# A two-layer backbone block on one core: order of routing, list loads and shared-expert steps

## The reference, cut to what matters

```python
def moe_ffn(h, w_router, router_bias, w_eg, w_eu, w_ed, w_sg, w_su, w_sd):
    scores = jax.nn.sigmoid((h @ w_router).astype(jnp.float32))
    # group-limited top-8 of 64, weights normalised, rows sorted by expert and padded to blocks of 128
    ...
    y = lax.map(expert_block, (row_tok.reshape(n_blocks, MOE_BLOCK), block_e)).reshape(n_rows, D)
    routed = jnp.zeros((T + 1, D), h.dtype).at[row_tok].add(y * row_w[:, None])[:T]
    shared = (jax.nn.silu(h @ w_sg) * (h @ w_su)) @ w_sd
    return routed + shared
```

## Time and profile before

| | |
|---|---|
| median of 3 runs | 3443.66 us (3431.37 to 3446.03) |
| the profiled execution | 3404.99 us, span 3403.1 us |
| PE busy | 3183.9 us (94%) |
| DVE, ACT, POOL busy | 1747.7, 1336.2, 595.3 us |
| chain that ended last, by engine | PE 68%, DMA 17%, DVE 5%, issue 4%, ACT 3%, POOL 1% |
| granted PE clock over the span | 0.981 |

### The profile page before, as it was taken

One profiled execution on the slowest core, in us unless ns is written; L12 is line 12 of the kernel. 1 busy time (PEld: TensorE's weight loads), 2 busy tenths in 40 slices (PEclk: granted clock), 3 DMA queues, 4 the chain that ended last, 5 costly groups with the idle time before them and its releaser, 6 DMA issues.

```text
span 3403.1 us, 47594 instructions
## 1 busy us (share of the span) xinstructions
PE 3183.9 (94%) x14840; PEld 2229.5 (66%) x14840; DVE 1747.7 (51%) x2409; ACT 1336.2 (39%) x1881; POOL 595.3 (17%) x751
## 2 busy tenths in 40 slices
PE   6999998999989999999998799999998899999996
PEld 3467866899645776667666346776764566776663
DVE  1344252133265766666675526342335666677665
ACT  2244152212122555555554225242212455555551
POOL 0000310000042332223332000020003222332220
PEclk9999999999999999999999999999999999999998
DMA  6310203333515999999996910103341899999986
GB/s 234 110 62 7 78 1 106 130 130 130 201 40 191 372 375 365 363 377 382 371 378 261 361 51 1 35 1 112 93 158 46 296 374 352 359 369 357 346 322 249
DMA packets 224802, 727.19 MB, mean 214 GB/s; under 512 B 55890, under 2 KB 104660, under 8 KB 165396
## 3 DMA queue, kind: packets, MB, share of 16 engines
q1 hardware_dynamic: 179508, 633.37, 50.6%
q0 software_dynamic: 45184, 92.28, 7.3%
HBM read 707.64 MB, written 84.24 MB: 233 GB/s over the span
## 4 chain that ended last, share of the span: by engine, by line
PE 68%; DMA 17%; DVE 5%; issue 4%; ACT 3%; POOL 1%; SPq 1%; DVEq 0%; POOLq 0%; ACTq 0%
PE ps L820 11%; PE ps L822 10%; PE ps L821 10%; PE ps L813 7%; PE ps L901 6%; DMA ring<-in_w_exp_up 6%; PE ps L842 5%; PE ps L1010 5%; DMA region_k<-in_w_exp_up 4%; PE ps L1112 4%; DMA region_v<-in_w_exp_up 3%; PE ps L1033 3%; DMA ring<-y_rows 2%; PE ps L929 1%; PE ps L1131 1%
## 5 line engine op out<-in xcount | busy, mean ns | idle before, releaser
L842 PEld LDWEIGHTS ps<-con,region_c 128*128 128x128 f32 x1878 | 249.0, 169 | 130.3 <-issue 90.8
L1967 POOL DMA_INDIRECT y_rows<-region_q,idx_out x141 | 147.3, 1045 | 892.2 <-DVE region_q L1572 806.4
L842 PE MATMUL ps<-con,region_c 128*128 128x128 f32 x1878 | 278.3, 277 | 22.0 <-DVE region_c L1803 8.7
L822 PE MATMUL ps<-region_x_split,ring_split 128*128 128x384 f32 (+2 forms) x800 | 283.9, 355 | 0.0
L820 PE MATMUL ps<-ring_split,region_q_split 128*128 128x512 f32 x568 | 227.9, 401 | 10.7 <-DVE ring_split L1539 8.7
L820 PE MATMUL ps<-region_h_split,region_q_split 128*128 128x512 f32 x560 | 225.1, 402 | 12.6 <-DVE ring_split L1539 11.7
L1190 ACT ACTIVATE region_q<-ps 128x512 f32<-128x512 f32 (+1 forms) x145 | 87.6, 604 | 366.7 <-PE ps L901 320.3
L822 PE MATMUL ps<-ring_split 128*128 128x512 f32 x568 | 222.6, 392 | 0.0
L822 PE MATMUL ps<-region_h_split,ring_split 128*128 128x512 f32 x560 | 220.1, 393 | 0.0
L1367 ACT ACTIVATE region_c<-ps 128x768 f32<-128x768 f32 (+1 forms) x48 | 33.8, 705 | 409.4 <-PE ps L822 409.4
L901 PE MATMUL ps<-region_k,region_c 128*128 128x512 f32 x384 | 172.8, 593 | 1.0 <-DVE region_c L1551 1.0
(11 more groups left out here) (312 smaller groups left out, 6886.0 us busy)
## 6 DMA issues: line engine op xcount, KB each, us to landing
ring<-in_w_mod SPq DMA_DIRECT2D x24, 2048.0 KB, 8.2
region_k<-in_w_exp_gate SPq DMA_DIRECT2D x48, 1024.0 KB, 7.4
region_k<-in_w_exp_up SPq DMA_DIRECT2D x48, 1024.0 KB, 16.8
region_k<-in_w_exp_down SPq DMA_DIRECT2D x48, 1024.0 KB, 15.3
ring<-in_w_exp_gate SPq DMA_DIRECT2D x47, 1024.0 KB, 7.6
ring<-in_w_exp_up SPq DMA_DIRECT2D x47, 1024.0 KB, 16.9
ring<-in_w_exp_down SPq DMA_DIRECT2D x47, 1024.0 KB, 15.3
region_v<-in_w_exp_gate SPq DMA_DIRECT2D x46, 1024.0 KB, 7.4
```

What stands on the lines that cost most here:

```text
L822: last = mm(o, wl, xh, start=False, stop=k == len(stationary) - 1)
L842: last = nc.tensor.transpose(ps[0:t.shape[1], at:at + t.shape[0]], t, ident[0:t.shape[0], 0:t.shape[0]])
L1967: pool.indirect_dma_start(Y8, bass.IndirectOffsetOnAxis(ap=idx_out[:, s:s + 1], axis=0), yb[:, s, :], None, bounds_check=TOK * TOPK - 1, o ...
```

## The change

In both layers, pieces 12 to 19 are split one `qs` step earlier (after `qs` 0 and 1, `qsp` 0 and 1, not after 1 and 2), and SP requests the first two merge panels before it waits for `rows`, not after. In both layers SP waits for the list stores and requests the lists ahead of the wait for the table and of all expert weights. Second layer: `r` of a tile stands before the next tile's `o`, `pos` directly a step later, POOL writes the lists two steps behind `keep_rows` rather than three, and the shared expert's jobs stand in a new order with `shift` last. First layer: the shared expert's jobs stand in a new order.

```diff
             if kind in ("qs", "qsp"):
-                return {1: [12, 13, 14, 15], 2: [16, 17, 18, 19]}.get(a[1], [])
+                return {0: [12, 13, 14, 15], 1: [16, 17, 18, 19]}.get(a[1], [])
...
-                load_until(("pm", l))
+                load_until(("merge", l, 1, 0))
                 sp.wait_ge(drained["dve"], names["rows", l].count)
...
                     spread("gt2", s, s_gt2)
+                sp.wait_ge(sl["listed"], 16 * TOPK * len(A))
+                sp.dma_start(slots, LISTS[l].rearrange("(p n) a -> p (n a)", p=P)).then_inc(sl["list_in"], 16)
                 sp.wait_ge(tab_ready, l + 1)
...
                 load_down(expert(1), 1)
-                sp.wait_ge(sl["listed"], 16 * TOPK * len(A))
-                sp.dma_start(slots, LISTS[l].rearrange("(p n) a -> p (n a)", p=P)).then_inc(sl["list_in"], 16)
                 sp.wait_ge(filled, names["sd", l, A[-1]].fill)
...
-                for n in range(len(A) + 3):
+                lag = 3 if l < DEPTH - 1 else 2
+                for n in range(len(A) + lag):
                     if n < len(A):
                         keep_rows(n)
-                    if n >= 3:
-                        list_tile(n - 3)
+                    if n >= lag:
+                        list_tile(n - lag)
```

More of the change, by code:

```diff
@@ L217, in make_plan @@
         assert not rest
+        router = dict(drain="act", panel=("router", l))
+        ahead = l == DEPTH - 1
         for i, t in enumerate(A):
+            if ahead and i >= 2:
+                add("r", l, A[i - 2], **router)
             add("o", l, t, drain="dve", panel=[("wo", l, 0), ("wo", l, 1)])
@@ L222, in make_plan @@
             add("norm", l, t)
[L223 to L227, removed]
-        add("f", l, A[-1], drain="act")
[L229 to L249, removed]
@@ L250, in make_plan, with shared @@
-        if l < DEPTH - 1:
+            if ahead and i >= 2:
+                add("pos", l, A[i - 2], drain="dve")
+            elif i >= 2:
+                add("r", l, A[i - 2], **router)
+                if i >= 3:
+                    add("pos", l, A[i - 3], drain="dve")
+        def shared(*steps):
+            for kind, n in steps:
+                add(kind, l, A[n], drain="act" if kind == "sT" else "dve")
+        if ahead:
+            add("r", l, A[-2], **router)
+        shared(("sg", 0))
@@ new lines, in make_plan @@
+        add("f", l, A[-1], drain="act")
+        if ahead:
+            shared(("pos", -2), ("sT", 0), ("sd", 0))
+            add("r", l, A[-1], **router)
+            shared(("sg", 1))
+        else:
+            add("r", l, A[-2], **router)
+            shared(("pos", -3), ("sT", 0), ("sd", 0))
+            add("r", l, A[-1], **router)
+            shared(("pos", -2), ("sg", 1), ("sg", 2))
+        shared(("pos", -1))
+        add("cnt", l, drain="dve")
+        shared(("sT", 1), ("sd", 1))
@@ L251, in make_plan @@
+        add("end", l, drain="dve")
+        shared(("sg", 2 if ahead else 3))
+        add("tab", l, drain="dve")
+        shared(("sT", 2), ("sd", 2))
+        if not ahead:
+            add("shift", l)
+            shared(("sg", 4), ("sT", 3), ("sd", 3))
+        add("first", l)
+        shared(("sg", -1))
+        if ahead:
+            add("shift", l)
+        else:
+            shared(("sT", -2), ("sd", -2))
             add("tok", l)
-        add("sT", l, A[-1], drain="act")
-        add("sd", l, A[-1], drain="dve")
@@ L254, in make_plan @@
-        if l == DEPTH - 1:
+        shared(("sT", -1), ("sd", -1))
+        if ahead:
             add("tok", l)
```

## The result

| timing | before, us | changed, us | difference | ratio, with its 95% interval |
|---|---|---|---|---|
| first | 3437.51 (4 runs) | 3377.52 (4 runs) | 60.0 | 0.9824 (0.9801 to 0.9846) |
| second (e5) | 3407.94 (19) | 3363.83 (4) | 44.1 | 0.9873 (0.9851 to 0.9895) |
| third (e10) | 3411.59 (28) | 3367.53 (4) | 44.1 | 0.9869 (0.9851 to 0.9886) |
| fourth (e14) | 3413.07 (9) | 3372.22 (2) | 40.9 | 0.9877 (0.9849 to 0.9906) |

A forecast was written before the change was run, and what follows sets the result against it. PE, busy 94% of the span, was taken as the bound, with gains from closing its gaps ahead of the expert loops: 14.0 + 14.8 + 5 + 6.5 = 40.3 us off the 3443.7 median gives 3403.4 us, range 3390 to 3423.

The forecast's parts named there:

- splits: Both layers, ahead of `u` 0: earlier splits close PE's gap and keep the clock up, 14.0 us (9.7 to 14.0).
- merge panels: Both layers, `pm` to `b`: earlier panel requests let `b` start as `pm` ends, 14.8 us (10.4 to 14.8).
- first layer's shared stage: First layer's shared expert jobs: new order fills PE's waits for `route` and `cnt`, 5 us (-3 to 8).
- second layer's routing and shared stage: Second layer: earlier list stores and list request end PE's wait for the lists sooner, 6.5 us (1 to 8).
- The 1.9 us that the prediction left at `r` 5: First layer's shared stage: a gap of about 1.9 us stays, as `r` 5 needs the slot of `pos` 3.
- waits of `r` 2 to 4: Second layer's routing: each waits for ACT's copy, about 4 us new; over 2 us each would show the prediction wrong.
- the walk through the queues to `pos` 5: Second layer's routing: places `pos` 5 at about 2622, so the last list store goes out at 2631, 10.7 us sooner.
- The bracket at `sT` 5: Second layer: `sT` 5 following a weight wait was a right sign; several us with a DMA behind, a wrong one.
- A: Rival: both shared stages give nothing, late expert weights or gathers replacing the gaps; 3414.9 us, chance 0.12.
- B: Rival: the early splits fail, through a late panel or another wait at `u` 0; 3417.4 us, chance 0.06.
- C: Rival: the expert loops lengthen, slower than before from 0.29 us a block; 3466.9 us at 0.45; chance 0.05.
- the last one, from the sum to the median: Whole kernel: 40.3 us taken off the 3443.7 median too, though the profiled execution lay an unplaced 38.7 us under it.

The follow-up runs named there:

- e5: The whole change again, against the kernel before: 3363.83 against 3407.94 us, ratio 0.9873.
- e10: The whole change again, on a third chip, against the kernel before: 3367.53 against 3411.59 us, ratio 0.9869.
- e14: The whole change once more, two runs, against the kernel before on the same chip: 3372.22 against 3413.07 us, ratio 0.9877.
- e11: First layer's new job order and lists ahead of expert weights, in the kernel before: 3406.44 against 3411.59 us, ratio 0.9982.
- e12: Second layer's new order with shorter list-store lag, and lists ahead of expert weights, in the kernel before: 3402.68 against 3411.59 us, ratio 0.9973.
- e1: The kernel before, unchanged, timed and profiled again: 3407.52 against 3408.39 us, ratio 0.9999.
- e13: The kernel before, unchanged, timed and profiled once more: 3411.22 against 3413.07 us.
- e6: Only the first layer's new job order, in the kernel before: 3411.64 against 3407.94 us, ratio 1.0019.
- e8: The whole change with `first` moved behind `sT` 5 in the second layer, against the kernel before: 3359.15 against 3407.94 us, ratio 0.9864.
- e3: The whole change without the earlier splits and merge panel requests, against the kernel before: 3390.45 against 3408.39 us, ratio 0.9948.
- e7: Only the second layer's new job order and shorter list-store lag, in the kernel before: 3405.24 against 3407.94 us, ratio 0.9992.
- e4: Only the lists requested ahead of the table and expert weights, in the kernel before: 3408.02 against 3408.39 us, ratio 0.9998.

## Why the prediction was right or wrong

**The sum.** The forecast's own range was 18 to 45 us of gain before the spread of the median; three later timings give 44.1, 44.1 and 40.9. Term by term:

| term | forecast, us | timed alone | in the stages |
|---|---|---|---|
| splits | 14.0 | 28.6 with the next | first layer 7.6 (forecast 7.56) |
| merge panels | 14.8 | | first layer 6.7 (6.57); second, both terms, 14.0 (14.70) |
| first layer's shared stage | 5 (-3 to 8) | 5.2 (e11) | 92.6 to 84.0: 8.6 |
| second layer's routing and shared stage | 6.5 (1 to 8) | 8.9 (e12) | 171.9 to 167.6: 4.3 |

The stage column takes means of the four profiles before and of e5, e10 and e14; its terms sum to 7.6 + 6.7 + 14.0 + 8.6 + 4.3 = 41.2. Against the one profile of before that the prediction was worked out from, the same differences are 7.7 + 6.1 + 14.4 + 7.0 + 5.1 = 40.3 us, the forecast itself. That is in part luck: the two shared stages are off by +2.0 and -1.4.

**Splits and panels: right.** Gap and clock went together, as summed: `u` 0 and `b` have no bracket and run at the durations of the full clock. What is lower behind a gap is again seen where one stayed: behind 4.89 us at `sT` 5 the eight matmuls of `sd` 5 take 5.15 us (2634.78), where they take 3.67 behind a gap of 0.56. By the Trainium skill's "TensorE: Matmul & The Clock Gate", section "What's actually happening", the point of transition varies from run to run; for the gaps removed here that mattered little, as the stage of the splits takes 102.9 to 103.4 us with its gap and 95.56 to 95.58 without. Elsewhere it mattered. In the second layer `sT` 2 starts 115.4 us behind the request for `w_out` in both e5 and e14. In e5 the `sg` 2 before it ran at a granted clock of 1.00, PE then idled 2.86 us, and `sd` 2 ran at 0.57; in e14 these are 0.84, 1.18 us and 1.00. `sd` 2 in e5, then in e14:

```profile
2576.32 6.38 PE L1160 MATMUL ps<-region_v,region_c 128*128 128x512 f32 x8 [0.56 <-ACT region_c L1205]
```

```profile
2576.75 3.67 PE L1160 MATMUL ps<-region_v,region_c 128*128 128x512 f32 x8 [0.57 <-ACT region_c L1205]
```

**First layer's shared stage: right in mechanism, under-sized by 2.0 us.** By the prediction the lists would be requested at 1040 to 1041 in before's time, expert 0 right behind. In e5 they are at 1026.99 and 1028.92; the stage begins 12.76 us earlier there (971.08 against 983.84), so 1039.75 and 1041.68. The expert weights were covered by `sg` 4 to `sg` 5 as reasoned: PE has no wait on a DMA in the stage, and the 3.07 us that ACT waits for them hold nobody up. PE's only bracket over 1.4 us is one of 3.30 ahead of `r` 4, which stood in the kernel before too (3.31 in e1). The 1.9 us that the prediction left at `r` 5 are not there: `sd` 0 covers them. With them the 5 us would have been 6.9, and from the profile of before (91.0 us) to the 84.0 it is 7.0. The 8.6 of the table are more because e1 and e13 are in its mean, at the lower clocks named with the stages. The experiments add what the prediction didn't weigh: this order alone wins nothing and is slower by 3.7 us as timed (e6). That the table comes later was noted there only as a cost for the weights; it also puts the lists behind them.

**Second layer: the wait moved, as said, and less was left over.** The waits of `r` 2 to 4 are 3.3 + 1.2 = 4.5 us, forecast 4. Behind them the chain runs as forecast, 2 to 5 us later. In before's time (the starts of `w_out` laid on 2492.13):

| step | forecast | e5 | e10, e14 |
|---|---|---|---|
| last list store | 2631 | 2635.9 | 2632.9, 2632.9 |
| lists requested | 2633 to 2634 | 2638.0 | 2635.1, 2635.1 |
| expert 0 requested | 2635.5 | 2640.5 | 2637.6, 2637.6 |
| PE behind its wait, at `sT` 5 | 2650.5 | 2654.1 | 2651.2, 2651.1 |

Against the 2656.98 of before, 2.9 us of the 6.5 are seen at this point in e5, and 5.8 and 5.9 in e10 and e14; in the first profile it is at 2657.3 and nothing is won. The mis-sized step is the walk through the queues to `pos` 5, put at 2622: POOL can store its rows at 2627.0 in e5 and at 2624.1 in e10 and e14. From e14 to e5 the difference is the slow `sd` 2 shown above. (The prediction calls the job at 2656.98 `sT` 4; by the order of the list it is `sT` 5, so it is the same job on both sides and the 6.5 stand.) PE waits for the second gather at `tok`, 1.52 us in the first profile, 1.42 and 1.36 in e5 and e10, and not at all in e14; the prediction only had 2 us less to spare there. The bracket at `sT` 5 was named, among the signs of right and also of wrong; it is 4.76 to 4.89 us, and e8 shows what makes it.

**Rivals.** A (the shared stages give nothing) falls by e3, 17.9 us; the late gathers of the first layer are not seen either, as `tok` waits 1.32 us for DVE before and after, and for no DMA. B falls by `u` 0, which has no bracket. C falls by the loops: 793.9, 792.6 and 794.5 us against 793.0 to 795.0, and 681.2, 679.8 and 683.2 against 679.3 to 683.4; a block would have had to be 0.29 us longer, 22 us in the first loop.

**The step that failed** is the last one, from the sum to the median: "So I take the same 40.3 off the median", with the 38.7 us between profile and median left unplaced and taken to fall on both kernels alike. It did not. Over the later timings the kernel before takes 3408 to 3413 us and the changed one 3364 to 3372; in the first, 3437.5 and 3377.5. So whatever made the first timing longer cost before 24 to 30 us and the changed kernel 5 to 14. The gain that the terms sum to is there, 41 to 44 us in the later timings; of the 25.9 us that the forecast missed by, 19.7 are the gain that only the first timing has, and 6.2 the starting value. The range, 54 us of gain at most, was built from the bounds of the terms and 5 us for the median, and had nothing for this.

What it was is only partly seen. The first profile of the changed kernel belongs to that timing, and its two shared stages, 89.63 and 172.3 us, are the longest of the four. There ScalarE starts late with no releaser on this core to name. ACT in the first layer, first profile, and then the same steps in e5:

```profile
1001.53 0.22 ACT L1405 ACTIVATE scores<-ps 128x64 f32<-128x64 f32 x1 [10.59 <-remote]
...
1011.56 0.38 ACT L1409 ACTIVATE region_c<-ps 128x256 f32<-128x256 f32 x1 [8.50 <-remote]
```

```profile
993.89 0.22 ACT L1405 ACTIVATE scores<-ps 128x64 f32<-128x64 f32 x1 [8.26 <-PE ps L1139]
...
1000.99 0.38 ACT L1409 ACTIVATE region_c<-ps 128x256 f32<-128x256 f32 x1 [5.57 <-PE ps L1146]
```

The same two steps are 2.3 and 2.9 us later behind their predecessors, and DVE and PE wait for them (PE 1.40 us at `sT` 1 and 2.78 at `sd` 1, against 0.55 and 0.61 in e5). No other profile has such a row, of either kernel. Why the kernel before lost more than twice as much there, and whether in these same places, stays open: no profile of it from that timing exists, and in no later timing did it take 3430 us. That the difference is one of chips is a guess: three chips gave 3408 to 3413, and which one the first timing ran on is not on record.

## What to carry to other kernels

An order of jobs and the order of a queue that serves them are one change: in the first layer the new order alone lost 3.7 us, the lists ahead alone won nothing, and together they won 5.2. When a step is moved, work out for every queue what now goes out ahead of what, and only then price the gap. And if a profile's own time doesn't lie among the timed runs, the unplaced difference is a term of its own, which need not be the same for both kernels, and the range must hold it.

## What the runs showed of the hardware that was not expected

- A load of the lists asked for right behind 6 MB of weights is usable 12.7 us (e6) and 13.1 us (e7) later; asked for some 12 us behind them it took 4.0 us (2647.64 to 2651.60), and with no weights asked for ahead of it 2.4 (e4 and e11, second layer). The Trainium skill, "Trainium Kernel Development and Optimization", section "Key Constraints", says that transfers from several engines' queues share the same 16 transfer engines. Here both transfers are SP's, so these rows add a price within one queue; whether POOL's gathers lost time to SP's weights no run here singles out.
- The same program took 3437.5 us in one timing and 3408 to 3413 in four others, while the changed one took 3377.5 and 3364 to 3372: the ratio of the first timing was off by 0.005 from that of the others, more than the 0.002 of its interval.
- The first 320 us of the kernel move by up to 8.6 us between profiles (315.3 to 323.9) whatever the change, while the stage behind them repeats to 0.02 us in four profiles of the changed kernel (95.56 to 95.58).
